# Feed-forward of a decoder trunk: twelve hidden tiles over all 512 tokens in place of one tile over 256

## The reference

```python
D_MODEL, SEQ, DEPTH, D_FF = 1024, 512, 2, 3072

def swiglu(x, w1, w3, w2):
    h = silu(x @ w1) * (x @ w3)        # x: 512 x 1024, w1 and w3: 1024 x 3072
    return h @ w2                      # w2: 3072 x 1024

h = x
for layer in range(DEPTH):
    h = h + hybrid_mixer(rms_norm(h, norm_mix_g[layer]), ...)
    hn = rms_norm(h, norm_ffn_g[layer])
    h = h + (swiglu(hn, ...) if layer % 2 == 0 else moe_swiglu(hn, ...))
return rms_norm(h, final_g)
```

## Time and profile before

| | |
|---|---|
| time, median of 3 runs (lowest to highest) | 2050.07 us (2049.92 to 2051.72) |
| span of the profiled execution | 2046.2 us |
| TensorE busy | 2005.7 us, 98% |
| VectorE busy | 1539.0 us, 75% |
| ScalarE busy | 1203.6 us, 59% |
| first matmul of the dense channel mixer | at 196.11 us |
| first matmul of `mixer(1)` | at 602.87 us |

### The profile page before, as it was taken

One profiled execution on the slowest core, in us unless ns is written; L12 is line 12 of the kernel. 1 busy time (PEld: TensorE's weight loads), 2 busy tenths in 40 slices (PEclk: granted clock), 3 DMA queues, 4 the chain that ended last, 5 costly groups with the idle time before them and its releaser, 6 DMA issues.

```text
span 2046.2 us, 33551 instructions
## 1 busy us (share of the span) xinstructions
PE 2005.7 (98%) x11091; PEld 1741.6 (85%) x11092; DVE 1539.0 (75%) x1701; ACT 1203.6 (59%) x1546; POOL 93.8 (5%) x139
## 2 busy tenths in 40 slices
PE   8999999999999998999999999999999999999997
PEld 7778888888888778999899988888999888889996
DVE  6896766666667986766677688898777698988785
ACT  4443555555555424655566577787665687877552
POOL 1000000100000002100100000000000000001000
PEclk9999999999999999999999999999999999999999
DMA  7321766766553313877687699999877799999871
GB/s 221 126 72 51 222 218 202 218 202 188 185 155 124 114 55 114 266 241 241 219 277 254 193 359 374 360 393 352 302 251 254 271 381 355 388 373 355 269 270 63
DMA packets 245416, 487.51 MB, mean 238 GB/s; under 512 B 16740, under 2 KB 86484, under 8 KB 245364
## 3 DMA queue, kind: packets, MB, share of 16 engines
q1 hardware_dynamic: 237812, 462.04, 66.8%
q0 software_dynamic: 7552, 24.80, 3.4%
HBM read 473.21 MB, written 13.58 MB: 238 GB/s over the span
## 4 chain that ended last, share of the span: by engine, by line
PE 91%; DVE 4%; issue 2%; ACT 1%; DMA 1%; POOL 0%; DVEq 0%; SPq 0%; ACTq 0%; POOLq 0%
PE PS L1587 89%; ACT whi L380 1%; PE PS L1950 1%; DVE wlo L763 1%; DVE OV L878 1%; PE PS L1619 0%; DMA raw<-in_expert_w 0%; DVE OV L892 0%; DVE OV L797 0%; PE PS L1849 0%; DMA OV<-x_tok,idx 0%; DMA OV<-in_norm_mix_g 0%; POOL SM L1404 0%; DVE RES L1378 0%; DMA raw<-in_w_in 0%
## 5 line engine op out<-in xcount | busy, mean ns | idle before, releaser
L763 DVE TENSOR_TENSOR wlo<-raw,whi 128x1024 fp32r<-128x1024 f32 x872 | 1031.6, 1221 | 201.3 <-ACT whi L380 193.9
L380 ACT ACTIVATE whi<-raw 128x1024 fp32r<-128x1024 f32 x872 | 888.0, 1053 | 252.7 <-PE PS L1587 161.7
L1587 PE MATMUL PS<-XN,whi 128*128 128x512 f32 (+3 forms) x3328 | 950.7, 363 | 11.3 <-issue 6.7
L1587 PE MATMUL PS<-XN,wlo 128*128 128x152 f32 (+3 forms) x2944 | 774.1, 263 | 0.0
L1587 PEld LDWEIGHTS PS<-XN,whi 128*128 128x128 f32 x3328 | 617.0, 188 | 74.0 <-issue 12.6
L1587 PE MATMUL PS<-whi,XN 128*128 128x512 f32 x2272 | 672.2, 394 | 4.3 <-issue 2.2
L1587 PEld LDWEIGHTS PS<-XN,wlo 128*128 128x128 f32 x2944 | 560.1, 190 | 15.6 <-issue 2.7
L1587 PEld LDWEIGHTS PS<-whi,XN 128*128 128x128 f32 x2272 | 423.9, 188 | 98.4 <-issue 6.9
L1587 PE MATMUL PS<-wlo,XN 128*128 128x512 f32 x1248 | 425.8, 391 | 0.0
L1587 PEld LDWEIGHTS PS<-wlo,XN 128*128 128x128 f32 x1248 | 234.4, 188 | 50.5
L1587 PE MATMUL PS<-whi,hid 128*128 128x512 f32 x384 | 111.6, 392 | 0.8 <-DVE hid L998 0.8
(11 more groups left out here) (242 smaller groups left out, 961.4 us busy)
## 6 DMA issues: line engine op xcount, KB each, us to landing
raw<-in_expert_w SPq DMA_DIRECT2D x672, 512.0 KB
raw<-in_ffn_w SPq DMA_DIRECT2D x144, 512.0 KB
raw<-in_w_in SPq DMA_DIRECT2D x40, 512.0 KB
raw<-in_w_out SPq DMA_DIRECT2D x16, 512.0 KB
y_rows<-OV POOLq DMA_DIRECT2D x13, 512.0 KB, 5.8
y_rows<-OV POOLq DMA_DIRECT2D x13, 192.0 KB, 6.8
RES<-in_x SPq DMA_DIRECT2D x4, 512.0 KB, 5.5
x_tok<-OV POOLq DMA_DIRECT2D x4, 512.0 KB, 2.9
```

The source lines that it names most:

```text
L380: act.activation(whi[:, u0 % CONV, half(h)], raw[:, r, half(h)], ACT.Copy).then_inc(s["hi_done"], 1)
L763: dve.tensor_tensor(wlo[:, w, half(h)], raw[:, u0 % RAW, half(h)], whi[:, w, half(h)].bitcast(F32), ALU.subtract).then_inc(s["lo_done"], 1)
L1587: return pe.matmul(out_, lhsT, rhs, start=start, stop=stop, skip_group_check=True)
```

## The change

The dense channel mixer is written anew. The hidden features are taken in two phases p = 0, 1 of 12 tiles. In a phase all 12 ups come first, over all 512 tokens, then the downs for tokens 0 to 255 (h = 0), then those for 256 to 511 (h = 1).

- An up pass is, for each slice of the contraction, three matmuls of 512 columns, all summed in PSUM; the copies and additions of before are gone. ScalarE's silu and VectorE's product read PSUM directly and are 512 wide.
- The gated values of 12 tiles are kept in slots 5, 0 and 1 of `whi` and `wlo`. The weights of this stage have slots 2, 3 and 4 alone.
- `w1` and `w3` are loaded once, `w2` twice: 48 units.
- The first four passes (tiles 0 and 1 of `w1` and `w3`) are run for tokens 0 to 255 first, then all four for 256 to 511, with `x_T(1, 3)` after the first two.
- The down of a unit is 24 matmuls of 512 columns. There is no loop on any engine.
- `mixer(1)` begins with its unit 2 not yet split, since slot 4 is in use until the last down. `mix_split(1, 2)` now stands after `second_norm`.
- `x_T(2, 0)` and `x_T(2, 1)` stand before the last down unit.

```diff
+FT = 12
+FPH = 4 * FT
+HID_SLOTS = (5, 0, 1)
         def mix_gate(eng, l, i):
...
             elif l > 0:
-                for n in ("w1_done", "w3_done", "w2_done"):
-                    eng.wait_ge(s[n], MOE_F)
+                ffn_free(eng, FPH - 3 + i if i < 3 else FPH - 1)
...
+        def slot(u):
+            return 2 + (u - FFN_BASE) % 3 if FFN_BASE <= u < MIX1_BASE else u % CONV
+        def up_bank(p, part, t):
+            return 4 * p + 2 * part + t
+        def down_bank(p, h):
+            return 4 if p == h else 0
...
@@ scalar
+            def ffn_split(v):
+                ffn_free(act, v - 3)
+                split(FFN_BASE + v, 0, 0)
+            def feed_forward():
+                for p in range(2):
+                    v0 = 2 * FT * p
+                    for g in range(FT // 2):
+                        ffn_silu(p, g, 0)
+                        ffn_silu(p, g, 1)
+                        ffn_split(v0 + 2 * g + 3)
+                        ffn_hi(p, g, 0)
+                        ffn_hi(p, g, 1)
+                        ffn_split(v0 + 2 * g + 4)
+                    for n in range(FT):
+                        if p == 0:
+                            ffn_split(v0 + FT + n + 3)
+                        elif n < FT - 1:
+                            ffn_split(v0 + FT + n + 3)
...
@@ vector
-                    for i in range(3, CONV):
+                    for i in range(2, CONV):
                         mix_split(1, i)
...
@@ tensor
-            def up(u0, du, f0, df, t, n, xo):
...
-                    for k in range(KD):
-                        mm(PS[:, bk, 0:2 * n], whi[:, w, a], XN[:, :, k, xo:xo + n], k == 0, False)
-                        ins = mm(PS[:, bk, 0:n], wlo[:, w, a], XN[:, 0, k, xo:xo + n], False, k == KD - 1)
...
+            def ffn_up(p, g, part, t, n0=0, n1=T):
...
+                if n0 == 0 and g:
+                    pe.wait_ge(s[("sl_done", "hm_done")[part]], n - 1)
+                for k in range(KD):
+                    mm(PS[:, bk, n0:n1], whi[:, w, a], XN[:, 0, k, n0:n1], k == 0, False)
+                    mm(PS[:, bk, n0:n1], whi[:, w, a], XN[:, 1, k, n0:n1], False, False)
+                    ins = mm(PS[:, bk, n0:n1], wlo[:, w, a], XN[:, 0, k, n0:n1], False, k == KD - 1)
...
+            def feed_forward():
+                for p in range(2):
+                    if p == 0:
...
+                        ffn_up(0, 0, 0, 0, 0, HALF)
+                        ffn_up(0, 0, 0, 1, 0, HALF)
+                        x_T(1, TB - 1)
+                        ffn_up(0, 0, 1, 0, 0, HALF)
+                        ffn_up(0, 0, 1, 1, 0, HALF)
+                        pe.wait_ge(s["xlo_done"], 8)
+                    else:
+                        pe.wait_ge(s["f_add"], 2)
+                    for g in range(FT // 2):
+                        for part in range(2):
+                            for t in range(2):
+                                ffn_up(p, g, part, t, HALF if p + g == 0 else 0)
+                    for h in range(2):
+                        if p:
+                            pe.wait_ge(s["f_add"], 4)
+                        for q in range(FT // 2):
+                            if p and h and q == FT // 2 - 1:
+                                x_T(2, 0)
+                                x_T(2, 1)
+                            ffn_down(p, h, q)
```

More of the change, by code:

```diff
@@ L308, in mixer_units @@
                     load(base_of[l] + 10 + i, 0, wout_v[l][:, 2 * o:2 * o + 2, :], 2)
[L310 to L314, removed]
+            def feed_forward():
+                for v in range(FPH):
+                    p, down, n = ffn_unit(v)
+                    if down:
+                        k = FT * p + 2 * (n % (FT // 2))
+                        load(FFN_BASE + v, 0, w2_v[:, k:k + 2, :], 2)
+                    else:
+                        c = FT * P * p + 256 * (n // 2)
+                        load(FFN_BASE + v, 0, (w1_v, w3_v)[n % 2][:, :, c:c + 256], KD)
             def expert(i, e):
@@ L379, in split @@
                     act.wait_ge(s[f"raw{r}{h}"], q * 16 + 16 * (u0 // RAW + 1))
-                    act.activation(whi[:, u0 % CONV, half(h)], raw[:, r, half(h)],
+                    act.activation(whi[:, slot(u0), half(h)], raw[:, r, half(h)],
                                    ACT.Copy).then_inc(s["hi_done"], 1)
@@ L530, in mixer @@
                 y_hi(l, 3)
[L532 to L553, removed]
@@ new lines, in feed_forward @@
+            def feed_forward():
[13 more added lines that the diff above has]
+                            ffn_split(v0 + FT + n + 3)
+                            if n == FT // 2:
+                                act.wait_ge(s["zero_out"], 1)
+                                for b in range(2):
+                                    act.wait_ge(s["y_evac"], b + 1)
+                                    squares(2 * TB + b, xa[:, b, :])
@@ new lines, in feed_forward @@
+            def feed_forward():
+                for p in range(2):
+                    v0 = 2 * FT * p
+                    for g in range(FT // 2):
+                        if p and g == 0:
+                            ffn_add(0, 1)
+                        ffn_split(v0 + 2 * g + 3)
+                        ffn_gated(p, g, 0)
+                        ffn_lo(p, g, 0)
+                        ffn_gated(p, g, 1)
+                        ffn_lo(p, g, 1)
+                        ffn_split(v0 + 2 * g + 4)
+                    for n in range(FT):
+                        if n == FT // 2:
+                            ffn_add(p, 0)
+                        if p == 0 or n < FT - 1:
+                            ffn_split(v0 + FT + n + 3)
+                        if p and n == FT // 2:
+                            mean(2 * TB)
+                            mean(2 * TB + 1)
+                            dve.wait_ge(s["gB_in"], 32)
+                            scaled(2 * TB)
+                            scaled(2 * TB + 1)
+                x_lo(2 * TB)
+                x_lo(2 * TB + 1)
+                ffn_add(1, 1)
@@ L2020, in _ @@
             mixer(0)
-            pe.wait_ge(s["xlo_done"], 6)
-            pe.wait_ge(s["res_done"], 4)
-            def last_turns():
-                x_T(2, 0)
-                x_T(2, 1)
-            for h in range(2):
-                channel_mixer(FFN_BASE + h * 3 * FFN_G, 0, F0 + h * 2 * FFN_G, 0, 2 * FFN_G, HALF, h * HALF,
-                              2 * h if h else None, early=None if h else lambda: x_T(1, TB - 1),
-                              between=last_turns if h else None)
+            feed_forward()
             mixer(1)
```

205 lines of the change are left out of this document (85 added, 120 removed).

## The result

The changed kernel takes 2078.39 us (median of 4 runs, 2076.87 to 2079.63), the kernel before in the same session 2050.89 (2049.92 to 2054.25): 1.0126 times as long, with a 95% interval of [1.0114, 1.0139]. (Ratios and intervals here are those on record; the quotient of two medians differs a little, 1.0134 in this case.) It is 27.5 us slower where 7.8 faster was forecast. The profiled execution has a span of 2078.0 us. Of all executions behind this document one was far off, 3275 us for the kernel with shift 43 and the convolutions first, at a mean granted clock of 0.556 where its others have 0.994 or 0.995; its ratio does without that one.

The account below looks back on a forecast made before the run. TensorE was taken to bound the dense channel mixer. Terms -7.9 - 1.0 - 1.2 + 2.3 = -7.8 us took the span from 2046.2 to 2038.4; plus 3.9 gave 2042.3 us, range 2039.5 to 2047.0.

Parts of the forecast that it names:

- Up passes, -7.9: Feed-forward (dense channel mixer): passes of 24 matmuls of 512 columns replace 16 pairs of 512 and 256, 7.9 us less.
- downs, -1.0: Feed-forward: 576 down matmuls of 512 columns take 0.227 us each where they took 0.2288, 1.0 us less.
- Stalls that go, -1.2: Feed-forward: TensorE's waits before the first down, between token halves and at the end go, 1.2 us less.
- The ring of three slots, 0: Feed-forward weight slots: a refill takes 3.5 us of 10.9 allowed, nothing charged; rival that it runs dry, 2059 us, chance 0.04.
- What is pushed, +2.3: Start of mixer(1): two more split halves on VectorE ahead of the convolutions delay TensorE's step 2, 2.3 us more.
- The rival with the clock: Step 2 of mixer(1): after 3.4 us idle TensorE's clock halves for 6.8 us, costing 3.4 us: 2045.7 us; chance 0.2.
- The mixers' and experts' work is untouched, and they start earlier by what is gained: Stages behind the feed-forward: no further term charged there; the gain of the sum, 7.8 us, carries through to the end.
- the 3.9 us that the sum adds to the span: Whole kernel: the median of before lies 3.9 us over its profiled span (2050.07 - 2046.2), added to the forecast span 2038.4.
- the -7.8 of the sum: Whole kernel: ups -7.9, downs -1.0, stalls -1.2 and pushed split +2.3 together, 7.8 us less.

Follow-up runs that it names:

- shift 43: Changed kernel with 43 semaphore increments added to VectorE's program ahead of the feed-forward, moving its expert loop from place 701 to 744: 2043.63 us, ratio 0.9963.
- the convolutions first: Changed kernel with VectorE's splits of units 3 to 5 of mixer(1) put behind the first two convolutions: 2079.4 us; with shift 43 too, 2046.55 us.
- shift 14: Changed kernel with 14 semaphore increments added to VectorE's program ahead of the feed-forward, moving its expert loop to place 715: 2043.07 us, ratio 0.9954.

## Why the prediction was wrong

- **Up passes, -7.9, and downs, -1.0: right.** Triples and downs start 0.227 us apart, as taken.
- **Stalls that go, -1.2: right.** TensorE has no idle in the stage. With all three the stage was forecast to go from 406.8 to about 396.5 us; it measured 395.7, 0.8 less.
- **The ring of three slots, 0: right.** No down matmul waits for a split; the ring did not run dry.
- **What is pushed, +2.3: right in mechanism, 0.4 short in size.** It measured +2.7 (3.93 less 1.23).
- **The rival with the clock came true.** It was priced at 3.4 us from a dip of 6.8; here the dip was 3.4 us long and cost 1.7. I gave it 0.2, taking 2.67 us without consequence as evidence against it, when the idle forecast was 3.4; in the experts of the changed kernel the clock fell behind 2.42 us. Later in `mixer(1)` TensorE's next wait grew from 0.34 to 0.70 us. With shift 43 it is 0.35, so this piece belongs to the placement too. That makes 2.7 + 1.7 + 0.36 = 4.8 of the 5.7 us of the table; the half clock around the router lasts 10.2 us in place of 6.8, which may be the rest.
- **The step that failed: "The mixers' and experts' work is untouched, and they start earlier by what is gained".** The work is untouched indeed, but the experts' loop of VectorE was moved by 85 instructions against the blocks in which its program is fetched, and cost 37.2 us. No term of the sum and no rival had a place for that. It is more than four times the whole gain that was forecast.

With that term taken out the rest stands up: shift 43 has 2043.6 and shift 14 2043.1, both inside the range of 2039.5 to 2047.0 around 2042.3. Their medians are 9.1 and 10.3 us under before in their sessions; their profiled spans (2041.3, 2043.4) are 4.9 and 2.8 us under the 2046.2. Medians and spans don't gain the same, because of the 3.9 us that the sum adds to the span: an execution takes 1.7 us more than its own span (2042.96 and 2041.3 with shift 43), so the profiled execution of before was itself some 2.2 us faster than the median. So the range holds them, though not quite for the reasons given: at the experts' first matmul the changed kernel was 5.4 us ahead, 2.4 less than the -7.8 of the sum, by the fall of the clock and the longer half clock around the router above all.

Could it have been seen? The place of the loop in VectorE's program stood in the built code of both kernels, and section 3 of the page of before has q14 with its 23 packets. What could not be read from before was that some places are slow: no jump of VectorE there waits longer than 1.5 us.

## What to carry to other kernels

A change that adds or removes instructions on an engine shifts every loop behind it; where a loop with branches is about as long as a few blocks of program code, its placement alone was worth 1.6 to 1.9% here (1.0126 against 0.9963, and 1.0193). When time appears in a part that was not edited, compare the packets of the instruction queues and the "issue" waits of each engine first, and try a few dozen instructions of padding before judging the change. And here a stall that was removed by reordering VectorE's queue came back at the next meeting points, and it went only when the work itself was put where VectorE is idle.

## What the runs showed of the hardware

- VectorE's program is fetched in blocks of 8192 bytes (all packets of q14 but a few small ones at the start), and the slow start of a loop of 271 instructions returned after 128 instructions (starts 701 and 829). The Trainium skill (Runtime: NRT & Kernel Launch, Instruction fetch mechanics) says that a taken branch whose target is outside the window of two blocks has to fetch it first. The traces agree that such a jump waits for a fetch, for 2.68 to 5.65 us; the page's block of 16 KiB isn't what this queue shows.
- TensorE's clock fell to its lower level behind 2.42 and 2.53 us of idle in the experts of the changed kernel and behind 2.25 us in the run with the convolutions first, and not behind 2.40 us in the changed kernel and 2.67 us in the one before.
- The loss at the jumps of VectorE becomes a second one on TensorE: in the experts 26.9 us of idle were followed by 9.5 us lost to the lower clock.
- A float32 matmul of 128 columns is recorded as two passes, 0.114 us each.
